# Taking the last two weight blocks of the first four down and output projections together, bank by bank

## What is computed

```
for i in range(2):
    y = mixer_i(rms_norm(x, norm_mix_pre[i]))            # ends in  ... @ w_out
    x = x + rms_norm(y, norm_mix_post[i])
    y = conv_geglu_ffn(rms_norm(x, norm_ffn_pre[i]))     # ends in  ... @ w_down
    x = x + rms_norm(y, norm_ffn_post[i])
```

## Time and profile before

| | |
|---|---|
| median of three executions | 2583.97 us |
| profiled execution, its own time | 2584.62 us |
| span of the program in it | 2582.8 us |
| TensorE busy with matmuls | 2557.0 us (99%), 12636 instructions |
| VectorE, ScalarE, GpSimd busy | 1662.8, 1273.6, 360.4 us |
| mean granted clock of TensorE | 0.999 |
| wraw<-in_w, the weight loads | 410, 512.0 KB each, median 3.4 us from issue to landing |
| the six largest groups on TensorE, L418 to L420 | mean 382 to 391 ns an instruction, started every 0.23 us |

### The profile page before, as it was taken

The page is one execution under the profiler, slowest core; times in us unless marked ns, Lnnn a source line. Parts: engine busy times, 40 slices in busy tenths (PEclk is TensorE's granted clock), DMA queues, the critical chain, the costliest instruction groups (busy, mean ns, idle before and its releaser), DMA issues.

```text
span 2582.8 us, 35280 instructions
## 1 busy us (share of the span) xinstructions
PE 2557.0 (99%) x12636; PEld 2031.7 (79%) x12636; DVE 1662.8 (64%) x2392; ACT 1273.6 (49%) x2133; POOL 360.4 (14%) x270
## 2 busy tenths in 40 slices
PE   9999999999999999999999999999999999999999
PEld 7855788888787557788888775799988777899887
DVE  4476677643988895677653777597633546687633
ACT  4326543333546895444333577577533425567432
POOL 0020100000103782100000130000610002000800
PEclk9999999999999999999999999999999999999999
DMA  5330223222243442232222230133232231332222
GB/s 215 106 94 25 96 98 97 97 94 95 83 134 121 136 132 74 80 99 97 97 98 97 92 103 4 56 125 99 84 110 97 92 105 50 98 123 99 82 97 98
DMA packets 74689, 250.44 MB, mean 97 GB/s; under 512 B 8748, under 2 KB 8876, under 8 KB 74192
## 3 DMA queue, kind: packets, MB, share of 16 engines
q1 hardware_dynamic: 73488, 240.63, 28.6%
q0 software_dynamic: 944, 8.33, 0.9%
q10 hardware_dynamic: 144, 0.00, 0.0%
HBM read 242.50 MB, written 2.24 MB: 95 GB/s over the span
## 4 chain that ended last, share of the span: by engine, by line
PE 91%; DVE 3%; ACT 2%; POOL 1%; issue 1%; SPq 0%; DMA 0%; DVEq 0%; ACTq 0%; POOLq 0%
PE bank L418 25%; PE bank L419 24%; PE bank L420 24%; PE bank L1316 2%; PE bank L1318 2%; PE bank L1317 2%; PE bank L2213 2%; POOL xT L863 1%; DVE mT L487 1%; PE bank L2765 1%; PE bank L3111 1%; PE bank L1661 1%; PE bank L1650 1%; PE bank L2220 1%; PE bank L2770 0%
## 5 line engine op out<-in xcount | busy, mean ns | idle before, releaser
L383 DVE TENSOR_TENSOR wlo<-wraw,whi 128x1024 fp32r<-128x1024 f32 x349 | 447.8, 1284 | 459.3 <-ACT whi L360 458.9
L360 ACT ACTIVATE whi<-wraw 128x1024 fp32r<-128x1024 f32 x353 | 371.7, 1055 | 515.4 <-DMA wraw<-in_w 515.4
L418 PE MATMUL bank<-hnhi,whi 128*128 128x512 f32 (+1 forms) x1528 | 596.3, 390 | 0.8 <-DVE wlo L383 0.5
L419 PE MATMUL bank<-hnlo,whi 128*128 128x512 f32 (+1 forms) x1528 | 584.5, 382 | 0.0
L420 PE MATMUL bank<-hnhi,wlo 128*128 128x512 f32 x1392 | 542.1, 389 | 0.0
L418 PE MATMUL bank<-ahi,whi 128*128 128x512 f32 x1184 | 463.5, 391 | 1.8 <-DVE stats L2874 0.6
L420 PE MATMUL bank<-ahi,wlo 128*128 128x512 f32 x1184 | 460.8, 389 | 0.0
L419 PE MATMUL bank<-alo,whi 128*128 128x512 f32 x1184 | 460.8, 389 | 0.0
L418 PEld LDWEIGHTS bank<-hnhi,whi 128*128 128x128 f32 x1528 | 287.2, 188 | 85.1 <-issue 29.1
L419 PEld LDWEIGHTS bank<-hnlo,whi 128*128 128x128 f32 x1528 | 287.4, 188 | 57.5 <-issue 3.4
L420 PEld LDWEIGHTS bank<-hnhi,wlo 128*128 128x128 f32 x1392 | 261.3, 188 | 55.6
(11 more groups left out here) (355 smaller groups left out, 3925.6 us busy)
## 6 DMA issues: line engine op xcount, KB each, us to landing
wraw<-in_w SPq DMA_DIRECT2D x410, 512.0 KB, 3.4
arena<-cs_scratch SPq DMA_DIRECT2D x20, 512.0 KB, 6.2
over_a<-cs_scratch SPq DMA_DIRECT2D x12, 512.0 KB, 6.2
arena<-in_rpb POOLq DMA_DIRECT2D x1, 2880.0 KB, 14.3
out_dram<-xT SPq DMA_DIRECT2D x8, 256.0 KB, 2.0
arena<-in_t_step POOLq DMA_DIRECT2D x2, 897.0 KB, 4.8
mT<-arena SPq DMA_DIRECT2D x28, 64.0 KB, 2.0
arena<-in_t_ab POOLq DMA_DIRECT2D x1, 1472.0 KB, 6.8
```

The lines of the kernel that those rows point to most:

```text
L360: act.activation(whi[:, slot * BLOCK:(slot + 1) * BLOCK], wraw[:, slot * BLOCK:(slot + 1) * BLOCK], ACT.Copy).then_inc(sem("w_hi"), 1)
L383: dve.tensor_tensor(low_home(i), wraw[:, slot * BLOCK:(slot + 1) * BLOCK], whi[:, slot * BLOCK:(slot + 1) * BLOCK], ALU.subtract).then_inc ...
L418: pe.matmul(out, wh, ah, start=start, stop=False)
L419: pe.matmul(out, wh, al, start=False, stop=False)
```

## The change

One line of `pe_down`: the first four projections take their last two blocks as the last four do. `last` is where the loop over whole blocks stops and the tail begins, and `skew` is K - 1 - `last`.

```diff
             if name in FIRST_ROWS:
                 pe_down_first(pe, name)
-            last = K - 1 if d < 4 else K - 2
+            last = K - 2
             for lo, hi in ((2, last),) if name in FIRST_ROWS else ((0, 1), (1, last)):
```

## The result

The changed kernel takes 2588.44 us, median of 20 executions (2587.28 to 2589.47), and the kernel before 2583.93 us in 20 executions (2582.01 to 2585.31). The ratio is 1.0017, with a 95% interval of 1.0011 to 1.0023: it is slower by 4.5 us, which is clear of noise, and just under the 0.2% that the forecast took as its bound. The profiled execution took 2589.15 us, with a span of 2587.4, 4.6 us longer than before's.

A forecast was written before the change was run, and what follows sets the result against it. TensorE, holding 91% of the chain that ended last, was taken to bound the kernel; early wait 1.80 plus late load 3.76 less 0.12 us gave +5.4 us, a forecast median of 2589.4 us, range 2587.0 to 2592.4.

The forecast's parts named there:

- the two costs: At the ends of the first four projections: an earlier input wait, 1.80 us, and a later weight load, 3.76 us.
- The products cost nothing, written out or not: The same 48 matmuls per projection, reordered, and the blocks written out in down0 and down1: no cost.
- Seven earlier banks: Squares and adds move into free time: worth nothing in ab_out, a gain of 0.12 us once in c_out.
- The early wait: TensorE waits for block K-1's input six products earlier: 0.45 us at each of four projections, 1.80 us in all.
- The late load: Block K+2's load, issued later, delays ScalarE's first half split 0.94 us at each of four boundaries: 3.76 us.
- The load in time: Rival: block K+2's load lands before the first half split, leaving +1.7 us, 2585.7 us; chance 0.05.
- The early banks pay: Rival: at the boundaries the split halves slip off the path, -2.3 us, 2581.7 us; chance 0.03.
- A load of 4.3 us: Rival: block K+2's load takes 4.3 us and lands 1.89 us late, +9.2 us, 2593.2 us; chance 0.08.
- The clock: Rival: TensorE's idling behind each projection halves its clock for 3.3 us, +12.0 us in all, 2596.0 us; chance 0.04.

The follow-up runs named there:

- the control: Kernel before's product order and waits, with the loop of down0 and down1 written out, against the kernel before: 2582.47 us against 2584.65, ratio 0.9995.
- four banks ahead: Changed kernel with block K-2 four banks ahead instead of two in the first four projections: 2583.01 us, ratio 0.9995 to the kernel before.
- the late load alone: Kernel before's order and waits, but SyncE holds block K+2's load until three products remain: 2585.92 us, ratio 1.0006 to the kernel before.
- three banks ahead: Changed kernel with block K-2 three banks ahead instead of two in the first four projections: 2583.95 us, ratio 0.9998 to the kernel before.
- the run with two transfers: Changed kernel with block K+2 loaded as two separately signalled 256 KB transfers: 2585.38 us, ratio 1.0006 to the kernel before.
- one bank ahead: Changed kernel with block K-2 one bank ahead instead of two in the first four projections: 2593.64 us, ratio 1.0037 to the kernel before.

## Why the prediction was right, point by point

The time lies in the range, 1.0 us under the forecast of 2589.4, and the mechanism was the one forecast: the two costs it named were each shown by a run of their own. Of the 1.0 us, 0.4 is in the boundaries (5.0 against 5.4, read below); the rest, 5.0 by the boundaries and 4.5 by the medians, is of the size of the wait in the latent attention, and isn't settled. The chances were put on the wrong side of the bound: 0.59 for over 0.2%, and it is 0.17%.

- *The products cost nothing, written out or not.* Right by the trace: 10.65 us for 48 in the control, and the stages between the boundaries are as long as before.
- *Seven earlier banks are worth 0.12 us.* Right in kind, shown by four banks ahead (1.66 us against 1.78). In the changed kernel it isn't a term of its own. At `c_out` the restart is 0.78 us late where L389 is 0.99 late, and this 0.1 us more than elsewhere stands for the gain; but the late load alone, with the banks as late as before, has it too (0.65 against 0.87). The sum had been late there anyway, and the late load hides that, with or without earlier banks.
- *The early wait, 0.45 us each.* 0.46 to 0.48 measured, and +1.40 for three when it was alone. That it all counts holds too: the restarts of that run are as early as before's.
- *The late load, 0.94 us each.* This is the term that was mis-sized. L389 did start 0.80 to 0.99 us later, 3.65 in all, but the restart only 0.71 to 0.87: 3.14 in all, where 3.76 less 0.12 was forecast. The part of it that failed is that "the second half, the logarithm and the exponential stand behind it" from the first moment on. The sum of squares on TensorE, for the first half of the positions, held the logarithm too. In the kernel before, its first six matmuls end at 284.13, and the logarithm starts at 284.17:

```profile
282.60 1.53 PE L812 MATMUL bank<-over_hn,base_t 128*128 128x256 f32 x6
```

  ScalarE starts an instruction about 0.1 us before the end of the one ahead when nothing holds it (285.21 against 285.30 in the changed kernel), and at 284.17 it did not: the halves could come 0.1 us later for nothing. With three banks ahead this is seen by itself: at `ab_out` the halves start 0.06 us later than before, and the logarithm at its old 1.64 us after the last square. Four times 0.1 is 0.4 us. The other 0.1 is the load: it took 3.18 to 3.35 us, mean 3.29, where 3.35 was taken. That is 0.24 us less for four, but each load went out 0.02 us later than the sum has it, and its first half was taken up 0.02 us after it had landed.

  The rule of the Trainium skill, "DMA: Bandwidth & Descriptors", section "Anatomy of one DMA — SWDGE (gpsimd) path", fitted for another issuing path, gave 3.2 us as an estimate for 512 KB: the four loads, at 3.18 to 3.35, were at it or up to 0.15 over. For 256 KB the same rule gives 2.6 us, again an estimate; in the run with two transfers 2.8 and 3.0 to 3.1 us were measured.
- *The rivals.* The load in time: no, but with four banks ahead it is. The early banks pay: no, ScalarE kept pace and still waited for the last one. A load of 4.3 us: the loads of K+2 took no more than 3.35; those of K+3 took up to 3.98, and had time for it. The clock: no fall at any of the four places (granted clock 1.00, the column behind the busy times below). The window behind `ab_out` shows TensorE busy for 5.11 of 6.40 us, more than the 4.63 of 6.34 that was worked out, since the window begins 0.2 us nearer to the sum of squares, and since the matmuls of no use (L820) no longer overlap that sum:

```profile
283.00:289.40 6.40, 5.11 (x23) 3.87 (x22) 4.81 (x12) 4.09 (x9) 0.00 (x0) 1.00 0.36 117
651.60:658.00 6.40, 5.19 (x23) 3.95 (x23) 4.89 (x11) 4.17 (x9) 0.00 (x0) 1.00 0.36 118
1074.30:1080.70 6.40, 5.19 (x22) 3.92 (x22) 4.71 (x11) 4.16 (x9) 0.00 (x0) 1.00 0.40 128
1443.10:1449.50 6.40, 5.18 (x22) 3.91 (x22) 4.72 (x11) 4.17 (x9) 0.00 (x0) 1.00 0.37 127
```

## What to carry to other kernels

Interleaving the last two steps of an accumulation finishes outputs earlier, but it takes the step's inputs earlier and frees its buffers later. Before doing so, look up who waits for the freed buffer and how long the load behind it takes: the products of the lead must last longer than the preparation of the next input (1.67 us here, from the first matmul of block K-2 to the one that waited), and the load must go out early enough to land before its turn. Here it took 3.2 to 3.4 us in most cases and its turn came 0.5 us after the last square, so it had to go out some 2.9 us ahead of that: three banks of lead gave 2.58 and were just short, four gave 3.26. Where the consumer already keeps pace with the producer, earlier outputs are worth next to nothing (0.12 us here). And when a chain shows an engine's own queue as what came last, look whether a second waiter ended at the same time: it sets how much of a new delay is free.

## What was not expected of the hardware

After a stall of the input TensorE doesn't resume at its pace at once: the second matmul follows the first by 0.34 us instead of 0.23, and a few of the next by 0.23 to 0.24, so that a wait of 0.31 us costs 0.45 to 0.48 in all. A load of 512 KB that follows another by 2.0 us took 3.3 to 4.0 us at the four boundaries, the one ahead of it 3.2 to 3.35; at two of the four it was no slower than before, when it followed by 5.4 us and took 3.2 to 3.5. Following by 1.4 us, with one bank ahead, it took 3.8 to 4.5 us at all four.

One transfer in a row of like ones took SyncE two to three times as long to issue (1.21 and 1.77 us where the rest took 0.59), and the load behind it was late by as much. And the fall of the clock is not worth the same everywhere: the stretch from 1540 to 1600 us is 1.6 to 1.7 us longer in the eight traces with a fall after 1555 us than in the three without one, but only 0.7 us longer in the profile of before, where the fall came at 1552.3. TensorE waited less behind it there, 1.42 us from one matmul to the next instead of 2.12.
